# Seven-product matmuls of two FFNs: the two pairs of output tiles alternate in the second phase, with other banks and more weight places

## The reference

```python
# first block: attention with differential and forgetting heads, then
h2 = rmsnorm(x, norm2_g)
g, u = h2 @ w_gate, h2 @ w_up              # 1024 -> 2816 each (22 tiles of 128)
x = x + (silu(g) * u) @ w_down             # 2816 -> 1024
# second block: convolutions and stick-breaking attention, then
h2 = rmsnorm(x, g_ffn)
x = x + square(relu(h2 @ w_ff1)) @ w_ff2   # 1024 -> 4096 (32 tiles) -> 1024
```

## Time and profile before

| what | us |
|---|---|
| median of 3 runs | 2466.11 (2465.25 to 2466.9) |
| the profiled execution | 2464.84 |
| its span | 2463.0 |
| TensorE busy | 2390.9 |
| VectorE busy | 1884.8 |
| GpSimd busy | 1326.5 |
| ScalarE busy | 1098.6 |

### The profile page before, as it was taken

How to read it: one execution, slowest core, us unless ns; L and a number is a source line. 1 busy time by engine, 2 the same in 40 slices (tenths; PEclk the granted TensorE clock), 3 DMA queues, 4 the chain that set the end, 5 groups by cost and what they waited for, 6 DMA issues and landing times.

```text
span 2463.0 us, 32007 instructions
## 1 busy us (share of the span) xinstructions
PE 2390.9 (97%) x11378; PEld 1950.7 (79%) x11378; DVE 1884.8 (77%) x2367; ACT 1098.6 (45%) x1885; POOL 1326.5 (54%) x887
## 2 busy tenths in 40 slices
PE   9999999999989999999999999999998999999998
PEld 7777788878768888877777878887876888778886
DVE  6777757673698778789879966777289888888966
ACT  6444556552533333354425436555263333543423
POOL 4666542211555555579845553331256555887862
PEclk9999999999999999999999999999998999999998
DMA  5311221132113233255412862223213444654522
GB/s 164 76 56 49 86 61 46 53 117 77 48 60 117 93 120 108 90 188 162 135 54 100 183 155 65 56 63 104 83 60 137 157 156 162 205 171 138 162 77 103
DMA packets 233260, 264.64 MB, mean 107 GB/s; under 512 B 18448, under 2 KB 145168, under 8 KB 232976
## 3 DMA queue, kind: packets, MB, share of 16 engines
q1 hardware_dynamic: 229504, 250.29, 32.3%
q0 software_dynamic: 3168, 11.54, 2.5%
q10 hardware_dynamic: 432, 0.79, 0.1%
HBM read 170.53 MB, written 61.60 MB: 94 GB/s over the span
## 4 chain that ended last, share of the span: by engine, by line
PE 76%; DVE 9%; POOL 7%; issue 4%; ACT 3%; DMA 2%; SPq 0%; POOLq 0%; DVEq 0%; ACTq 0%
PE PS L1768 21%; PE PS L1773 21%; PE PS L1770 21%; PE PS L1866 3%; PE PS L1853 2%; PE PS L1887 2%; PE PS L1884 2%; POOL lows L2626 2%; POOL R L2635 2%; PE PS L1847 2%; DVE R0f L2173 1%; DVE X L2257 1%; DVE R L2249 1%; PE PS L1850 1%; DVE values L2151 1%
## 5 line engine op out<-in xcount | busy, mean ns | idle before, releaser
L1768 PE MATMUL PS<-R,wh 128*128 128x512 f32 x2860 | 1138.8, 398 | 29.1 <-DVE stage L2161 12.4
L2626 POOL TENSOR_TENSOR lows<-values,wh 128x512 fp32r<-128x512 f32 (+2 forms) x483 | 725.5, 1507 | 774.5 <-ACT wh L2378 625.3
L1773 PE MATMUL PS<-R,wh 128*128 128x512 f32 x2860 | 1121.6, 392 | 8.7 <-DVE R L2180 5.9
L1770 PE MATMUL PS<-R,lows 128*128 128x512 f32 x2496 | 977.9, 392 | 5.6 <-POOL lows L2626 5.4
L1768 PEld LDWEIGHTS PS<-R,wh 128*128 128x128 f32 x2860 | 540.8, 189 | 148.3 <-DVE X L2257 15.5
L1773 PEld LDWEIGHTS PS<-R,wh 128*128 128x128 f32 x2860 | 540.2, 189 | 129.1 <-DVE R L2180 7.2
L2378 ACT ACTIVATE wh<-values 128x512 fp32r<-128x512 f32 (+2 forms) x484 | 299.3, 618 | 585.6 <-PE PS L1773 560.9
L1770 PEld LDWEIGHTS PS<-R,lows 128*128 128x128 f32 x2496 | 471.3, 189 | 99.9 <-POOL lows L2626 9.4
L2257 DVE TENSOR_TENSOR X<-PS,X 128x1024 f32<-128x1024 f32 x168 | 204.3, 1217 | 72.2 <-PE PS L1773 69.8
L2626 POOL TENSOR_TENSOR late_r<-late,wh 128x512 fp32r<-128x512 f32 (+1 forms) x92 | 138.7, 1509 | 76.7 <-ACT wh L2378 39.1
L2161 DVE TENSOR_TENSOR stage<-PS,stage 128x512 f32<-128x512 f32 x156 | 105.6, 685 | 64.6 <-PE PS L1773 64.3
(11 more groups left out here) (279 smaller groups left out, 3205.4 us busy)
## 6 DMA issues: line engine op xcount, KB each, us to landing
scr_hid<-R1f SPq DMA_DIRECT2D x177, 256.0 KB, 2.9
R0f<-scr_hid SPq DMA_DIRECT2D x92, 256.0 KB, 3.4
values<-w_in_dram SPq DMA_DIRECT2D x88, 256.0 KB, 2.9
R1f<-scr_hid SPq DMA_DIRECT2D x85, 256.0 KB, 3.4
values<-w_ff_dram SPq DMA_DIRECT2D x62, 256.0 KB, 3.0
values<-w_ff_dram SPq DMA_DIRECT2D x100, 128.0 KB, 2.4
R<-R SPq DMA_DIRECT2D x96, 128.0 KB, 2.3
X<-X POOLq DMA_DIRECT2D x22, 512.0 KB, 5.8
```

What stands on the lines that cost most here:

```text
L1768: e.matmul(PS[:, b, :], wh, high, start=s["start"], stop=False, skip_group_check=on)
L1770: e.matmul(PS[:, b, :], wl, high, start=False, stop=False, skip_group_check=on)
L1773: m = e.matmul(PS[:, b, :], wh, low, start=False, stop=s["stop"], skip_group_check=on)
L2626: e.tensor_tensor(T.wl[piece.v][:, 0:m], T.wv[piece.v][:, 0:m], T.wh[:, piece.h, 0:m].bitcast(F), ALU.subtract).then_inc(*sg.up("w_lo", pi ...
```

## The change

- The seven products of the two sides alternate: P1 of side 0, P1 of side 1, P2 of side 0, and so on. Each side has two pairs of banks of its own, which change their parts from chunk to chunk.
- The weight pieces of a chunk are listed for both sides together, with both a12 and the sums s4 made from them at the end; 14 places are needed.
- The five stages 0 to 4 become weight places 9 to 13 when the last pair has been made, and are given back behind the last block product. Each is free as a place when its last hidden tile is made.
- Operand rows of the next chunk are fetched after each two products.
- Block_in is listed at the seventh and ninth pair, one side each, in place of ahead of the first pair. What it waits for stays.
- During the pairs dense_banks is set to a list of all eight banks and dense_at to a value by their number. dense_seven and its counter are not in the diff. In the first FFN dense_at is 4 as before, in the second 6 in place of 4, so that dense_last begins with bank 7 and bank 4.

Cut from the diff: a function that gives the semaphores of the five new places a name (those of the stages), its uses in the loads, and an assertion.

```diff
@@ Tiles
-        self.wv += [late[:, i, :] for i in range(2)]
-        self.wl += [late_r[:, i, :] for i in range(2)]
+        self.wv += [late[:, i, :] for i in range(2)] + self.stage[0:5]
+        self.wl += [late_r[:, i, :] for i in range(2)] + self.stage_r[0:5]
@@ Order.plan_blocks
-    def plan_blocks(self, name, e, k, n):
-
-        kind, m = f"block{n}", 2 * n
-        a11 = self.plan_piece(kind, name, e, k, m, False, turn=False)
-        a21 = self.plan_piece(kind, name, e + 1, k, m, False, turn=False)
-        a22 = self.plan_piece(kind, name, e + 1, k + 1, m, False, turn=False)
-        a12 = self.plan_piece(kind, name, e, k + 1, m, False, turn=False)
-        s1 = self.plan_piece("sum", "minus both", 0, 0, m, False, (a21, a22), False)
-        s2 = self.plan_piece("sum", "minus both", 0, 0, m, False, (s1, a11), False)
-        s3 = self.plan_piece("sum", "in place", 0, 0, m, False, (a11, a21), False)
-        s4 = self.plan_piece("sum", "difference", 0, 0, m, False, (a12, s2), False)
...
-        for product in BLOCKS:
-            self.plan_turn(factors[product])
-        return factors
+    def plan_blocks(self, name, k, rows):
+
+        kind, m, sides = f"block{rows}", 2 * rows, []
+        for e in (0, 4):
+            a11 = self.plan_piece(kind, name, e, k, m, False, turn=False)
+            a21 = self.plan_piece(kind, name, e + 1, k, m, False, turn=False)
+            a22 = self.plan_piece(kind, name, e + 1, k + 1, m, False, turn=False)
+            s1 = self.plan_piece("sum", "minus both", 0, 0, m, False, (a21, a22), False)
+            s2 = self.plan_piece("sum", "minus both", 0, 0, m, False, (s1, a11), False)
+            s3 = self.plan_piece("sum", "in place", 0, 0, m, False, (a11, a21), False)
+            sides.append(dict(P1=a11, P6=s2, P5=s1, P7=s3, P4=a22))
+            a11.read_by, a22.read_by, s1.read_by = [s2, s3], [s1], [s2]
+        for e, side in zip((0, 4), sides):
+            a12 = self.plan_piece(kind, name, e, k + 1, m, False, turn=False)
+            s4 = self.plan_piece("sum", "difference", 0, 0, m, False, (a12, side["P6"]), False)
+            a12.read_by, side["P6"].read_by = [s4], [s4]
+            side.update(P2=a12, P3=s4)
+        for product in BLOCKS:
+            for side in sides:
+                self.plan_turn(side[product])
+        return sides
@@ constants
-BLOCK_BANKS = [dict(P1=b, P6=b, P7=b, P5=b, P2=4, P4=6, P3=6) for b in (0, 2)]
+BLOCK_BANKS = [[dict(P1=b, P6=b, P7=b, P5=b, P2=c, P4=c, P3=c) for b, c in pairs] for pairs in (((0, 4), (2, 6)), ((4, 0), (6, 2)))]
+SEVEN_BANKS = [0, 1, 4, 5, 6, 7, 2, 3]
+BLOCK_IN = (6, 8)
@@ ffn
-        O.dense_banks = [3, 4, 5, 6, 7]
+        O.dense_banks, O.dense_at = SEVEN_BANKS, -7 * len(factors) % 8
...
-        for g in range(2):
-            O.step("block_in", tag=tag, g=g, given=whole)
...
         for i in range(len(factors)):
             order = SEVEN if i else SEVEN_FIRST
             gen = O.dense_seven((tag, i), order, factors[i], 1, 0, evacs(i), None if i else first_ready(tag))
+            if i in BLOCK_IN:
+                O.step("block_in", tag=tag, g=BLOCK_IN.index(i), given=whole)
...
+        for i in range(5):
+            O.v_free.append((9 + i, O.stage_given[i]))
+            O.stage_given[i] = None
         for c, (k, rows) in enumerate(todo):
             here = operands(c)
+            products = []
             for g in range(2):
...
-                for name in O.dense_blocks(t, blocks[k, g], rows, here, operand_ready, BLOCK_BANKS[(2 * c + g) % 2], evac):
-                    if g:
-                        for n in here[name]:
-                            free[n] = [O.last_dense]
-                    elif c + 1 < len(todo):
-                        fetch_block(c + 1, name)
-                    else:
-                        x = BLOCKS.index(name)
-                        if x % 2 == 0:
-                            fetch_plain(x // 2)
+                products.append(O.dense_blocks((tag, "blocks", c, g), blocks[c][g], rows, here, operand_ready, BLOCK_BANKS[c % 2][g], evac))
+            for x, name in enumerate(BLOCKS):
+                for g in range(2):
+                    next(products[g])
+                for n in here[name]:
+                    free[n] = [O.last_dense]
+                if c + 1 < len(todo):
+                    fetch_block(c + 1, name)
+                elif x % 2 == 0:
+                    fetch_plain(x // 2)
...
+        for v, events in [place for place in O.v_free if place[0] > 8]:
+            O.stage_given[v - 9] = events
+        O.v_free = [place for place in O.v_free if place[0] < 9]
```

More of the change, by code:

```diff
@@ L264, in __init__, with raw @@
         self.qk_done = self.pv_done = self.rotated = None
+def raw(v):
+    return f"raw{v}" if v < 9 else f"st{v - 9}"
 class Piece:
@@ L275, in made @@
     def made(self):
-        return ("w_sum", self.n) if self.kind == "sum" else (f"raw{self.v}", self.n)
+        return ("w_sum", self.n) if self.kind == "sum" else (raw(self.v), self.n)
 class Order:
@@ L380, in plan_group @@
             self.plan_piece("group", *tiles[0], k, rows * len(tiles), sources=tuple(tiles))
-    def plan_blocks(self, name, e, k, n):
-        kind, m = f"block{n}", 2 * n
-        a11 = self.plan_piece(kind, name, e, k, m, False, turn=False)
-        a21 = self.plan_piece(kind, name, e + 1, k, m, False, turn=False)
-        a22 = self.plan_piece(kind, name, e + 1, k + 1, m, False, turn=False)
-        a12 = self.plan_piece(kind, name, e, k + 1, m, False, turn=False)
-        s1 = self.plan_piece("sum", "minus both", 0, 0, m, False, (a21, a22), False)
-        s2 = self.plan_piece("sum", "minus both", 0, 0, m, False, (s1, a11), False)
-        s3 = self.plan_piece("sum", "in place", 0, 0, m, False, (a11, a21), False)
-        s4 = self.plan_piece("sum", "difference", 0, 0, m, False, (a12, s2), False)
-        a11.read_by, a22.read_by, a12.read_by = [s2, s3], [s1], [s4]
-        s1.read_by, s2.read_by = [s2], [s4]
-        factors = dict(P1=a11, P6=s2, P2=a12, P5=s1, P7=s3, P3=s4, P4=a22)
+    def plan_blocks(self, name, k, rows):
[14 more added lines that the diff above has]
+            side.update(P2=a12, P3=s4)
         for product in BLOCKS:
-            self.plan_turn(factors[product])
-        return factors
+            for side in sides:
+                self.plan_turn(side[product])
+        return sides
     def plan_seven(self, first, second):
@@ L1058, in plan_ffn @@
                 O.plan_turn(factors[i][name])
-        blocks = {(k, g): O.plan_blocks(down, 4 * g, k, rows) for k, rows in chunks(tiles) for g in range(2)}
+        blocks = [O.plan_blocks(down, k, rows) for k, rows in chunks(tiles)]
         for e in range(8):
@@ L1443, in ffn @@
         added = {}
+        for i in range(5):
+            O.v_free.append((9 + i, O.stage_given[i]))
+            O.stage_given[i] = None
         for c, (k, rows) in enumerate(todo):
             here = operands(c)
+            products = []
             for g in range(2):
-                t = (tag, "blocks", c, g)
                 def evac(name, b, event, c=c, g=g):
@@ L1470, in ffn @@
         O.dense_banks = [3, 4, 5, 6, 7]
-        assert {7, 8} <= {v for v, _ in O.v_free}
+        for v, events in [place for place in O.v_free if place[0] > 8]:
+            O.stage_given[v - 9] = events
+        O.v_free = [place for place in O.v_free if place[0] < 9]
+        assert {7, 8} <= {v for v, _ in O.v_free} and None not in O.stage_given[0:5]
         given_back = [event for v, events in O.v_free if v > 6 for event in events] + O.return_stages(MIDDLE) + [last_block]
@@ L2725, in sync_program @@
                     e.dma_start(dst, weights[c + 2 * i, :, k:k + 2 * rows - 1:2, :]).then_inc(
-                        *sg.up(f"raw{piece.v}", piece.n if i else (piece.n, i), by=16))
+                        *sg.up(raw(piece.v), piece.n if i else (piece.n, i), by=16))
                 continue
@@ L2735, in sync_program @@
                     dst = T.wv[piece.v][:, i * rows * 128:(i + 1) * rows * 128].rearrange("p (k c) -> p k c", c=128)
-                    e.dma_start(dst, args[name][c, :, k:k + rows, :]).then_inc(*sg.up(f"raw{piece.v}", piece.n if i == len(piece.sources) - 1 else (piece.n, i), by=16))
+                    e.dma_start(dst, args[name][c, :, k:k + rows, :]).then_inc(*sg.up(raw(piece.v), piece.n if i == len(piece.sources) - 1 else (piece.n, i), by=16))
                 continue
@@ L2743, in sync_program @@
             dst = dst.rearrange("p (k c) -> p k c", c=128)
-            e.dma_start(dst, src).then_inc(*sg.up(f"raw{piece.v}", piece.n, by=16))
+            e.dma_start(dst, src).then_inc(*sg.up(raw(piece.v), piece.n, by=16))
         elif kind == "mask_load":
```

## The result

The changed kernel takes 2471.76 us in the median of 16 runs (2470.45 to 2473.45), the kernel before 2466.9 (16 runs, 2463.77 to 2472.86): ratio 1.002, interval 1.0012 to 1.0027. It is 4.9 us slower, inside the range of the forecast (2451 to 2473), but on the other side of no change: a gain of 6.3 us was forecast, and the prediction was wrong.

What follows compares the result with a forecast made beforehand. TensorE, busy 2390.9 of 2463.0 us, was taken as the bound, so only its stops and slow clock could change. A -7.0, B -4.3, C +5, D 0, E 0 gave -6.3 us: forecast 2460 us, range 2451 to 2473.

Steps and rivals of the forecast that it cites:

- A: Second phases and their seams: with alternating sides and own banks, waits for bank-emptying adds go, 1.7 us left; -7.0 us.
- B: Second phases: operand rows fetched evenly level GpSimd's queue, so waits for weight low parts shrink; -4.3 us.
- C: Second-phase entries: bank wait stays, second side's place and stages late; first FFN +5 us (-2.5 to +12), second 0.
- D: First pairs: listing the residual rows later moves nothing, since the planner reorders; 0 us, ends -11 and +3.
- E: End of the second phase: first side's closing operations, now after the last product, stay hidden; loads unchanged; 0 us.
- Rival 3: Entry costs more than the phase gains: a12 and its sum wait for last pair's stages; +8, 2474 us; chance 0.18.
- The signs of being wrong: Wrong if residual rows moved, the first block product does not wait, or the third waits over 8 us.
- 2 + 2.6 + 3.3 + 2.3: Forecast cost of the first FFN's second-phase entry, given as 10.5 us in place of 5.5.

Runs made afterwards that it cites:

- e9: On e3, all chunks alternating, stages the last pair doesn't use become weight places ahead of it: 2462.66 us, ratio to the kernel before 0.9986.
- e4: On the changed kernel, the first chunk of each FFN runs side 0's seven products ahead of side 1's: 2462.72 us, ratio to before 0.9984.
- e1: On the kernel before, only the residual rows (block_in) listed later, at pairs 6 and 8, conditions unchanged: 2467.13 us, ratio 1.0003.
- e2: As e1 on the kernel before, with block_in also waiting for the last add of the pair ahead of it: 2457.2 us, ratio 0.9962.
- e3: On the changed kernel, the last products begin with bank 4 in both FFNs: 2467.75 us, ratio to the kernel before 1.0003.
- e6: On the changed kernel, each side's closing operations also wait for the other side's last adds: 2465.45 us, ratio to the kernel before 1.0003.

## Why the prediction was wrong

- **A and B, right.** Every X wait inside the phases and most of the low-part waits there went. Together, and without the first seam, they were forecast at -12.2 (-7.9 and -4.3). Measured were -8.5 inside the first FFN's phase, -4.4 inside the second's and -0.9 at the second seam, 13.8 in all; the stretches do not part A from B.
- **C, the step that failed by its size.** The three things were named rightly: the last pair add is still waited for, at 3.20 and 2.07 us, since the counter was left as it is; the second side's sums are late; the stages are late (e9). But "three sums of 0.7 to 1.8 us mixed with other VectorE work ... about 7 us" was 13.5 us: the low part is finished at 1100.85, the pair product ended at 1087.3. So the stop at the second block product, put at "some 2.5 us", was 7.07 and 5.61. The three sums themselves are as long as said (1.76, 0.67 and 0.68 us); what was put too low is the other VectorE work ahead of and between them. By the timeline that is, in the first FFN, the scalings and hidden products that free the stages, and the first block add; in the second, scaled relus, operand subtractions and the first block add. This order is read from the trace and no run turned it round alone; that the sums' place and the alternation together make the stop is shown by e9 and e4. The stop of 3.3 us at the third block product did not come in the changed kernel. Forecast +5 and 0, measured +7.8 and +5.1.
- **D, right and shown** by e1. Moving the step in the list moves nothing; e2 shows the prize that was left lying, 9.3 us.
- **E, wrong.** "The first side's closing two operations now come after the last product ... 0." They come ahead of the last add, since they become ready one product earlier, and the queue doesn't know that a bank waits. Against the 0.8 us that this seam cost before, the 1.7 that A left there were +0.9; it came to +5.5, and e3 and e6 take it away in two ways. This is the second step that failed.
- **Rival 3** had the right sign and the right place (entry of the second phase, VectorE's queue) and the wrong carrier: the sums of the second side, not a12. It put 12 and 5 us on the two entries; 7.8 and 5.1 were enough with the seam.
- **The signs of being wrong** did not show: the residual rows had not moved, the first block product waited, and the third had no wait of 8 us. They watched the rows and the third product, and the loss was at the second product and at the seam. That the time fell inside the stated range is owed to the range's width and not to the sum.
- **Two readings.** The 1687 ns median of the earlier trace rows is that of the 45 subtractions into R from R0f; the 43 from R1f have a median of 679 ns in the same trace, so 1.69 is not the median of the line as a whole. And 2 + 2.6 + 3.3 + 2.3 is 10.2, not 10.5. Neither changes the account.

By the parts, from the forecast's -6.3 to the profiles' +7.5 (13.8 us): the entries took 7.9 more than forecast, the first seam 4.6, the second block 3.6 and the start 0.4; the phases with the second seam gave 1.6 more than forecast (13.8 for 12.2), and the second FFN's first pair 1.2.

At the first entry a sum takes 1.76 us at 1094.42, beside GpSimd subtractions, and 0.67 us at 1097.24, with GpSimd idle from 1097.3. The prediction named the exclusive lock between VectorE and GpSimd (the Trainium skill, "SBUF — State Buffer", section "SBUF: two separate sides") as what would bring term C to its upper end. The trace agrees that operations beside GpSimd's are longer; the entry, at +7.8, came to lie between the forecast's +5 and the upper end of +12, and no run shows how much of it is the lock.

## What to carry to other kernels

When two streams of work are interleaved to give each more time between its steps, look at the first round: what the second stream needs ready is asked for half a round earlier, and here that cost about as much as the steady state gave (12.9 against 13.8 us). Moving an entry in the list that this planner reorders moved nothing; a condition did. Edits that each take one of two waits in the same place can give more together than their sum. And before an operation is called hidden behind the end of a phase, see what in the same queue it can get ahead of.

## What the hardware showed beside that

The length of a stop alone does not tell whether the lower clock follows. After 2.07 us of waiting at 2130.25 the matmuls start 0.43 us apart (2130.76, 2131.19); the granted clock from 2130.3 to 2133.7 is 0.51, the lower of the two levels (1.2 GHz). In the kernel before, after 2.45 us at 1270.25, they go on 0.23 us apart, and the granted clock from 1270.3 to 1275 is 1.00. Before either stop TensorE had worked without a wait at a granted clock of 1.00 (2110 to 2127.8, and 1250 to 1267.4). At the second entry of the kernel before the lower clock cost 2.9 us beside the wait: 14 steps from 2123.64 to 2129.75 take 6.11 us where 14 of 0.227 would take 3.18.
